# Key tiles cut as quarters of four pages, with scales turned by VectorE, in a one-core MLA and RWKV-7 step

## What is computed

```python
def _decompress(c_kv, w_ukv, g_kn):
    kv = jnp.einsum('btc,chd->bthd', c_kv, w_ukv)
    return _rmsnorm(kv[..., :NOPE], g_kn), kv[..., NOPE:]
...
    def step(carry, phys):
        c_blk = cache_ckv[layer, phys]
        kp_blk = cache_kpe[layer, phys]
        kn_blk, v_blk = _decompress(c_blk, w_ukv, g_kn)
        return _merge(carry, _attn_partial(qn, qp, kn_blk, kp_blk, v_blk, None)), None
    carry, _ = lax.scan(step, init, page_table.T)
```

## Time and profile before

| | us |
|---|---|
| median of 3 runs | 1277.22 |
| lowest, highest | 1276.84, 1281.60 |
| profiled execution | 1276.86 |
| span of its trace | 1275.1 |
| PE busy, DVE busy, ACT busy | 1202.1, 732.2, 426.5 |

### The profile page before, as it was taken

One profiled execution on the slowest core, in us unless ns is written; L12 is line 12 of the kernel. 1 busy time (PEld: TensorE's weight loads), 2 busy tenths in 40 slices (PEclk: granted clock), 3 DMA queues, 4 the chain that ended last, 5 costly groups with the idle time before them and its releaser, 6 DMA issues. The chain is left out here.

```text
span 1275.1 us, 23690 instructions
## 1 busy us (share of the span) xinstructions
PE 1202.1 (94%) x8783; PEld 661.3 (52%) x8783; DVE 732.2 (57%) x1801; ACT 426.5 (33%) x1041; POOL 257.4 (20%) x294
## 2 busy tenths in 40 slices
PE   6999999989999999999989988999999999989898
PEld 3545677745565565655434445555444444454343
DVE  4000437955667666774768787888676667430331
ACT  3000354323343333342444343333444444210310
POOL 0000134711011121234412340001323232000000
PEclk9999999999999999997999999999999999999999
DMA  6413112123232222351453226532576544101000
GB/s 219 168 55 87 35 33 67 53 59 80 66 81 67 76 73 77 84 115 42 124 143 88 76 74 171 168 80 74 153 184 172 139 122 123 50 1 38 17 21 33
DMA packets 205236, 114.45 MB, mean 90 GB/s; under 512 B 152977, under 2 KB 196433, under 8 KB 204994
## 3 DMA queue, kind: packets, MB, share of 16 engines
q1 hardware_dynamic: 198482, 96.56, 27.7%
q0 software_dynamic: 4352, 10.49, 3.3%
q10 hardware_dynamic: 2288, 5.89, 1.3%
HBM read 75.79 MB, written 4.07 MB: 63 GB/s over the span
## 5 line engine op out<-in xcount | busy, mean ns | idle before, releaser
L563 PE MATMUL PS<-wk,c_T 128*128 128x512 f32 x1024 | 494.5, 612 | 13.5 <-DVE c_T L673 12.4
L563 PEld LDWEIGHTS PS<-wk,c_T 128*128 128x128 f32 x1024 | 180.3, 193 | 207.8 <-issue 162.8
L686 DVE TENSOR_REDUCE ssq<-PS 128x8 f32<-128x512 f32 x256 | 176.3, 689 | 169.7 <-ACT PS L609 156.8
L609 ACT ACTIVATE PS<-PS 128x512 f32<-128x512 f32 x256 | 150.3, 587 | 271.8 <-PE PS L563 245.0
L1557 PE MATMUL PS<-xnT,w_ring 128*128 128x276 f32 x416 | 101.0, 400 | 0.0
L1395 PE MATMUL PS<-w_ring,xnT 128*128 128x424 f32 x256 | 96.4, 534 | 0.9 <-DVE xnT L1041 0.9
L673 DVE STREAM_TRANSPOSE c_T<-blocks 128x512 f32<-128x512 f32 x126 | 88.3, 701 | 3.7 <-DMA blocks<-c_ring 3.2
L1557 PEld LDWEIGHTS PS<-xnT,w_ring 128*128 128x128 f32 x416 | 77.8, 190 | 20.6 <-issue 4.1
L489 POOL DMA_INDIRECT c_ring<-in_cache_ckv,token_rows x48 | 45.3, 944 | 182.1 <-PE PS L547 174.8
L480 POOL DMA_INDIRECT r_ring<-in_cache_kpe,group_rows x64 | 62.0, 969 | 92.3 <-DVE r_T L681 68.0
L1395 PEld LDWEIGHTS PS<-w_ring,xnT 128*128 128x128 f32 x256 | 48.8, 194 | 45.5 <-issue 45.4
(11 more groups left out here) (535 smaller groups left out, 1725.3 us busy)
## 6 DMA issues: line engine op xcount, KB each, us to landing
blocks<-c_ring SPq DMA_DIRECT2D x504, 64.0 KB
c_ring<-in_cache_ckv SPq DMA_DIRECT2D x208, 128.0 KB, 2.2
w_ring<-in_w_in SPq DMA_DIRECT2D x4, 1696.0 KB, 12.4
w_ring<-in_w_in SPq DMA_DIRECT2D x9, 512.0 KB, 5.1
w_o<-in_w_out SPq DMA_DIRECT2D x8, 512.0 KB, 4.9
w_g<-in_w_ple_gate SPq DMA_DIRECT2D x8, 512.0 KB
xn<-in_x_prompt SPq DMA_DIRECT2D x4, 512.0 KB, 10.9
w_ring<-in_w_in SPq DMA_DIRECT2D x2, 1024.0 KB, 6.1
```

Source lines behind the costliest of these rows:

```text
L563: mm = pe.matmul(PS[:, NORM[v % 2], :], c_T[:, u % 2, k, t * P:(t + 1) * P], wk[:, k], start=(k == 0), stop=(k == 1))
L609: nc.scalar.activation(PS[:, NORM[v % 2], :], PS[:, NORM[v % 2], :], ACT.Square).then_inc(no_sb, 1)
L686: dve.tensor_reduce(ssq[:, u % 2, t * H:(t + 1) * H], PS[:, NORM[v % 2], :].rearrange("p (h c) -> p h c", h=H), AX.X, ALU.add).then_inc(re ...
```

## The change

A tile becomes a quarter of all four pages of the step. The page copy lays token `s*32+g` of a page on partition `4g+s`; the transposes then leave column `s*128 + t*32 + g` of `c_T` for token `s*32+g` of page `t`. Tile `s` holds tokens `32s` to `32s+31` of each page. So each 32-partition block of a tile's `ssq` belongs to one page, and the transposes of 32 x 32 blocks that DVE makes put the scales on the right rows: `rep`, its transpose on PE and ACT's copy of the product go, and DVE writes `scale_T` and reads the product from PSUM. Columns of `dots` are picked by a stride, and `r_T` is written with a step of four.

Every tile now needs both halves. DVE turns half a in slot 2 and half b in slot 3 of the step before, and SP's pieces with the blocks are queued one slot sooner. On DVE the scales follow the first slot's sum, and the scores move from slot 2 to slot 1; on ACT the exponentials move from slot 3 to slot 2.

```diff
-                                  io["cache_ckv"][bass.ds(number, 1)].rearrange("o p c -> (o p) c")
+                                  io["cache_ckv"][bass.ds(number, 1)].rearrange("o (s g) c -> (o g) s c", s=GT)
...
             def dots(u):
                 pe.wait_ge(tn_sb, u + 1)
-                if u >= 1:
-                    pe.wait_ge(hi_sb, u)
...
-                                       c_T[:, u % 2, k, t * P:(t + 1) * P], start=(k == 0), stop=(k == 1))
+                                       c_T[:, u % 2, k, :].rearrange("d (q t i) -> d t q i", q=GT, t=GT)[:, t],
+                                       start=(k == 0), stop=(k == 1))
...
-                if t == 2 and u >= 1:
-                    turn_scale(u - 1)
                 norms(u, t)
...
-                if t == 1:
-                    dotted(u)
-                if t == 3 and u >= 1:
+                if t == 2 and u >= 1:
                     weights(u - 1)
                 square(u, t)
...
-                dve.transpose(r_T[:], r_ring[:, u % R_RING, :]).then_inc(tn_sb, 1)
+                dve.transpose(r_T[:].rearrange("d (g s) -> d s g", s=GT),
+                              r_ring[:, u % R_RING, :].rearrange("d (s g) -> d s g", s=GT)).then_inc(tn_sb, 1)
...
-                dve.tensor_tensor(rep[:].rearrange("p (x t) -> p x t", t=TS),
-                                  y.rearrange("p (x o) -> p x o", o=1).to_broadcast(wide),
-                                  tmp.rearrange("p (x o) -> p x o", o=1).to_broadcast(wide), ALU.mult).then_inc(scale_sb, 1)
+                LA(dve.tensor_tensor(tmp, y, tmp, ALU.mult))
+                LA(dve.transpose(scale_T[:], tmp.rearrange("p (x o) -> p x o", o=1).to_broadcast([P, GT * H, TS])))
...
-                if t == 0:
+                if t == 1:
+                    if u >= 2:
+                        merge(u - 2)
                     if u >= 1:
-                        turned_blocks(u, 1)
-                        scales(u - 1)
-                if t == 1 and u >= 2:
-                    merge(u - 2)
-                if t == 2 and u >= 1:
-                    score(u - 1)
-                if t == 3 and ahead:
-                    turned_blocks(u + 1, 0)
+                        score(u - 1)
+                if t >= 2 and ahead:
+                    turned_blocks(u + 1, t - 2)
                 reduce(u, t)
+                if t == 0 and u >= 1:
+                    scales(u - 1)
                 if t == 1 and ahead:
                     turned_r(u + 1)
...
-        on_sp = Stream(pages_sp(), lambda slot: 4 if slot <= PREP_SLOTS else min(2 * NSTEP, (slot + 6) // GT + (slot + 3) // GT + 2))
+        on_sp = Stream(pages_sp(), lambda slot: 4 if slot <= PREP_SLOTS else min(2 * NSTEP, (slot + 6) // GT + (slot + 4) // GT + 2))
```

More of the change, by code:

```diff
@@ L101, in shape_constants @@
     parts += [("headones", (s // HN == t // HN))]
-    parts += [("lane", s % 32), ("token", s)]
+    parts += [("lane", s % 32), ("token", s % 4 * 32 + s // 4)]
     parts += [("mod32", (s % 32 == t % 32))]
@@ L252, in build @@
         score_s = place("score_s", [P, 2, P])
-        rep = place("rep", [P, GT * QH])
+        scale_T = place("scale_T", [P, P])
         ew_q = place("ew_q", [P, P])
@@ L498, in pages_requested, with by_quarter @@
             return min(NSTEP, slot // GT + R_RING) + max(0, min(NSTEP, (slot + 6) // GT + 1) - GATHERED)
[L500 to L503 removed]
+        def by_quarter(k):
+            return (c_T[:, 0, k, :].rearrange("d (s t g) -> d t s g", s=GT, t=GT),
+                    PS[:, TURN, :].rearrange("d (t g s) -> d t s g", s=GT, t=GT))
         def pages_pe():
@@ L530, in dots, with turn_weights @@
                         mm = pe.matmul(PS[t * QH:(t + 1) * QH, TURN, at + P:at + 2 * P], qp[:, k, u // STEPS, :],
-                                       c_T[:, u % 2, k, t * P:(t + 1) * P], start=(k == 0), stop=(k == 1))
+                                       c_T[:, u % 2, k, :].rearrange("d (q t i) -> d t q i", q=GT, t=GT)[:, t],
+                                       start=(k == 0), stop=(k == 1))
                 mm.then_inc(rp_ps, 1)
-            def turn_scale(u):
-                pe.wait_ge(scale_sb, u + 1)
+            def turn_weights(u):
+                pe.wait_ge(eq_sb, u + 1)
                 if u >= 1:
                     pe.wait_ge(acc_sb, u)
-                pe.transpose(PS[:, MISC, at_t], rep[:], ident).then_inc(scale_ps, 1)
-            def turn_weights(u):
-                pe.wait_ge(eq_sb, u + 1)
                 pe.transpose(PS[:, MISC, at_t], ew_q[:], ident).then_inc(ew_ps, 1)
@@ L557, in norms @@
                         pe.wait_ge(lo_sb, u)
-                if t == 2 and u >= 1:
-                    pe.wait_ge(hi_sb, u)
+                        pe.wait_ge(hi_sb, u)
                 if v >= 2:
@@ L585, in pages_pe @@
             yield
-            turn_scale(NSTEP - 1)
             yield
@@ L597, in turned_first @@
                 act.wait_ge(k_ps, 1)
-                nc.scalar.copy(*by_token(0)).then_inc(k_sb, 1)
-            def dotted(u):
-                act.wait_ge(rp_ps, u + 1)
-                if u >= 2:
-                    act.wait_ge(eq_sb, u - 1)
-                nc.scalar.copy(score_s[:, u % 2, :], PS[:, TURN, u % 2 * 2 * P + P:u % 2 * 2 * P + 2 * P]).then_inc(np_sb, 1)
+                nc.scalar.copy(*by_quarter(0)).then_inc(k_sb, 1)
             def square(u, t):
@@ L668, in turned_first @@
                 dve.wait_ge(k_ps, 2)
-                dve.tensor_copy(*by_token(1)).then_inc(k_sb, 1)
+                dve.tensor_copy(*by_quarter(1)).then_inc(k_sb, 1)
             def turned_blocks(u, half):
                 dve.wait_ge(block_in[half], 64 * u)
-                dve.transpose(c_T[:, u % 2, :, 2 * half * P:2 * (half + 1) * P].rearrange("d x (t s p) -> d s t x p", t=2, s=GT),
+                dve.transpose(c_T[:, u % 2].rearrange("d x (s t g) -> d s t x g", s=GT, t=GT)[:, :, 2 * half:2 * half + 2],
                               blocks[:, half, :].rearrange("p (s t c x) -> p s t x c", s=GT, t=2, x=2)
@@ L689, in scales @@
             def scales(u):
-                wide = [P, GT * H, TS]
                 y, tmp = rms[:, 0, :], rms[:, 1, :]
```

12 lines of the change are left out of this document (4 added, 8 removed).

## The result

The changed kernel takes 1300.03 us (1298.84 to 1303.07) beside 1278.97 of the kernel before in the same measurement: ratio 1.0166, 95% interval 1.0141 to 1.0191. It is slower, by some 21 us, and outside the predicted range of 1262 to 1283. The span of the profiled execution went from 1275.1 to 1297.1 us.

The account below looks back on a forecast made before the run. PE was taken to bound the kernel before the attention, PE and DVE nearly full in it, SP's queue the tail. From 1276.86 us, -6.7 - 4.1 - 1.6 + 1 + 7 - 0.5 = -4.9 gave 1272 us, range 1262 to 1283.

Parts of the forecast that it names:

- The tail, forecast -0.5: Tail: SP's step stays 9.29 us, its run begins 1.9 us earlier, first norm ends -0.3, last transpose 0.2; -0.5 us.
- rival B: Tail: scattered page copy slows SP's queue; +12.6 us at 0.6 more a step, ending at 1284; chance 0.18.
- over the tail SP is the slower one: Tail: SP's queue takes 9.29 us a step, the loop through PE, ACT and DVE 9.04.
- The attention, forecast +7: Prompt's attention: moved scores, scales and exponentials land 0.9 us a step on PE over eight steps; +7 us.
- the first, the scales: Prompt's attention, DVE: scores wait behind slot 0's sum and the scales, ending 0.43 us past slot 1's possible sum.
- the second, the exponentials: Prompt's attention, ACT: exponentials stand ahead of slot 2's squares, which come 0.5 us later a step.
- Rival A: Prompt's attention loses nothing: +7 becomes -1.7 us, the kernel takes 1263 us; chance 0.33.
- The barrier, forecast nothing: Barrier before the prompt's attention: SP's blocks ahead of it add 2.7 us, hidden in SP's 5.3 us of standing; no cost.
- Up to the attention, forecast -11.4: Before the prompt's attention: PE's transposes -6.7, dots' waits -4.1, `turn_scale`'s wait -1.6, added DVE work +1 us.
- The term for PE's work: Before the attention: 32 transposes of the scales leave PE at 0.21 us each; -6.7 us.
- The terms of -4.1 and -1.6 for waits: PE's waits before the tail: half of the dots' 8.3 us for half b goes, and `turn_scale`'s 1.6 for `merge`.
- Rival C: DVE's writes of `r_T` by 16-byte steps run at half speed, 0.6 us for 0.3; +5 us, 1277; chance 0.07.

Follow-up runs that it names:

- flat: The changed kernel with the page copy reading one contiguous run and rotary keys written in runs again; 1.0054 of the kernel before.
- best_ba: flat_all3 with, from step 40 on, half b's blocks ahead of half a's on SP and DVE turning b first; 0.9875 of the kernel before, 1253.4 us.
- flat_all3: flat with scales ahead of slot 0's sum, exponentials back in slot 3 and SP's blocks a slot later; 0.9959 of the kernel before.
- flat_sp3: flat with SP's blocks asked a slot later again, at (slot + 3); 1.0022 of the kernel before.
- before_scattered: The kernel before with only the page copy's source changed, to rows of 1 KB, 32 KB apart; 1.0074 of the kernel before.

## Why the prediction was wrong

**The tail, forecast -0.5, measured +15.4.** This step failed, and it is rival B, which I gave 0.18. "What changes for SP is where its run begins and ends", and against B: "pieces stay 1 KB each and their number stays". I counted the pieces that land and not what SP does to hand out the copy. Landing did not change: SP waited 31.9 us in 20 waits for pages before and 31.5 in 20 after. Issue did, 0.43 to 0.69 us a copy, and that was enough: 0.5 us a step is double the 0.25 from which B was to decide. The Trainium skill's row that I had set against B (DMA: Bandwidth & Descriptors, Latency and other measured facts) gives rates of copies between HBM tensors at pitches of 512 KiB and more; a pitch of 32 KB and the time of issue lie outside it, so it spoke neither for B nor against. The price itself was well inside B's own scale (12.6 at 0.6 a step; 9.6 to 10.0 measured at 0.52 to 0.54). The error was its chance. Rows of one form of a copy can't price another form, and here SP was already the slower loop.

**The other third of the tail, 5.8 us in flat.** The tail can be split at SP's blocks, and these are flat's of step 43 and of the last step:

```profile
887.35 5.96 SPq L451 DMA_DIRECT2D blocks<-c_ring  x8
...
1078.47 5.94 SPq L451 DMA_DIRECT2D blocks<-c_ring  x8
```

| us | before | flat | after |
|---|---|---|---|
| row 42 to blocks of step 43 | 2.75 | 1.05 | 1.08 |
| 20 steps of SP | 185.71 | 191.12 | 201.17 |
| last blocks to row 63 | 3.75 | 5.82 | 5.36 |

The start came 1.7 us earlier, for the 1.9 forecast, and the end took 2.1 us more, since half b is issued 2.66 behind half a. These two were in my sum, together near nothing, and so they are. What I had not was SP's step: 9.56 for 9.29 with the same issue times, 5.4 us in all. Its wait for the pages grew only from 1.60 to 1.72 us. The gathers on POOL go out at 1053.16 to 1055.67 in flat, so that the last is still being issued when the pages go at 1056.29, where before they ended 2 us ahead of them. That they collide is argued, not shown. In best_ba, where SP issues the gathered half while the pages land, the time between SP's page copies and its next blocks fell from 2.02 us (flat_all3) to 1.49, most of the 0.64 that its step lost; that speaks for the landing as the cause, but the run also changed which half PE waits for.

My reading "over the tail SP is the slower one" also needs a limit. It was so in the mean. Step by step, 16 of before's 21 steps of PE in the tail lasted 9.03 to 9.05 us, the time of the loop through DVE, and SP's slower mean was mostly taken up by slack. In flat PE's steps run from 8.87 to 10.53 us, in after most from 9.65 to 10.5. DVE's waits for blocks point the same way: 3.2 us before, 10.1 in flat, 19.8 in after. So what the change took away, beside SP's time, is that slack; that it came from starting a step on half a is my reading of the order, and no run tests it alone.

**The attention, forecast +7, measured +5.7.** Size and sign held: 15.93 us a step for the 16.1 forecast, and PE's waits for the exponential 1.65 us a step for 1.6 (13.2 us in eight steps, before 5.9). The 1.3 us between forecast and measured are near the 1.6 by which PE's work fell in this stretch (114.8 to 113.1 us), which I had counted as lost in a wait. Of its two mechanisms the first, the scales, is confirmed at 0.39 us a step, near the 0.43; the second, the exponentials, was 0.16 and not 0.5. The slower rotary transpose and the scattered source together added 0.08 of the 0.71 a step (after against flat). Rival A is dead.

**The barrier, forecast nothing, measured +4.3.** "SP's blocks ahead of two stores and of the stage's barrier (SP stood 5.3 us at that barrier, the blocks add 2.7)" stood among the edits at no cost. It failed in two ways: the other engines came to this barrier earlier than before (PE ended its work 2.1 us behind row 33 and not 4.2), so SP's slack was gone, and SP had all eight copies, 5.42 us, and their waits ahead of it, not 2.7. Flat_sp3 gives 2.8 of it back. The rest stands beside the slower norm products behind the barrier, 3.62 us for 1.88. The sooner blocks alone, in the kernel before, were not tried: SP would stand ahead of the barrier for a half that DVE turns only behind it.

**Up to the attention, forecast -11.4, measured -4.9** at row 33. The term for PE's work held: 5.7 us less for 6.7. The terms of -4.1 and -1.6 for waits came to nothing: the dots' 8.3 us of waits and `turn_scale`'s 1.6 went, but PE met new ones, 3.0 more for the prompt's `nat`, 3.8 in issue waits of the norms, 2.3 more ahead of the `q_all` products (line 2295), 1.6 more for `pa`, 1.2 at an earlier barrier, and only its waits for `c_T` fell, by 2.3. Its idle time stayed where it was. In the later measurements the same stretch is 7.8 us shorter in flat and 10.1 in flat_all3 than in before_scattered, 4.0 and 7.8 of it idle time of PE. So most of that gain shows there without the repairs; why the first measurement shows only 5.3 us is open.

**Rival C** was half right. The transpose with a step of 16 bytes took 399 ns for 301, a third more and not twice. The Trainium skill (SBUF — State Buffer, Door 1: The DMA port swizzle) says a crossing to a new 16-byte line pays a penalty; the trace agrees, with 98 ns more for this transpose. With the scattered source it adds 0.6 us in the attention (126.4 against 125.8).

Sum by the stretches: -4.9 + 4.3 + 5.7 + 15.4 + 1.4 = +21.9 for a span that grew by 22.0.

## What to carry to other kernels

When a queue is the slower of two loops, price the issue of each copy on it as well as the landing; if the change gives a copy another form, the rows of the old form are no price, and the range has to be open on that side. Before a layout is bought, ask whether both sides can keep the order they have: here neither the scattered page nor the stepped transpose was needed. Put work where the engine waits for another, not where another waits for it, and look at each barrier for what the queue now carries ahead of it.

## What the runs showed of the hardware

- A copy of 128 pieces of 1 KB takes SP 0.43 us to issue with a contiguous source (before, flat) and 0.69 to 0.70 with rows 32 KB apart (after, before_scattered), each half of a pair's time; SP's wait for the pages to land was the same (31.9 and 31.5 us in 20 waits).
- A DVE transpose of 128x128 fp32 takes 301 ns writing runs, 399 with a step of 16 bytes, and 311 reading each value four times.
- Behind the barrier of the attention four norm products took 1.88 us in before (PE had stood 3.00), 3.62 in flat_sp3 (3.69), and 3.62 in after and flat (6.27 and 6.15); in before_scattered the granted clock behind 3.01 us of standing was 0.72 over 6 us, and they took 3.25. Standing as long as before did not bring the same clock back. In flat_all3 the first product behind 3.95 us of standing took 0.46 us as in before, and the norms after it 3.34.
